# RWKV-7 mixing in chunks of 64 tokens instead of 32, and a reordered VectorE queue in sparse attention

## The chip, the cores and the metric

One core of a Trainium2 chip runs the whole network. The metric is the device time of one execution in microseconds (us), median of the runs. TensorE is called PE in the profile, its weight loads PEld, VectorE is DVE, ScalarE is ACT, GpSimd is POOL and SyncE is SP.

## The reference

A trunk of four layers over 256 tokens of width 1024, float32 in and out. Each layer adds a token mixer's output to the residual stream and then a conv-gated MLP's. The mixers are: layers 0 and 3 sparse attention, layer 1 RWKV-7, layer 2 a state-space layer. Two of them matter here.

Sparse attention: a light indexer (8 heads) scores keys for each query, the best 64 keys are kept, and 16 heads of 64 dimensions attend to those only, causal in blocks of 64. The softmax is over the kept keys.

RWKV-7: for each of 16 heads a 64x64 state goes through the tokens:

```python
sa = einsum('bhij,bhj->bhi', state, -kk_t)
state = state * w_t + sa[..., None] * (kk_t * a_t) + v_t[..., None] * k_t
y = einsum('bhij,bhj->bhi', state, r_t)
```

## The kernel before

Everything is float32 and lies in SBUF with features on the partitions. The dense products split weights and activations into a rounded part and a rest (x_high, x_low) and add three matmuls (`product`, L371 to L373). A weight tile goes through the ring in SBUF; ACT rounds it (`round_weights`, L346), and DVE (half 0) and POOL (half 1) compute the rest (`rest_of_weights`, L354). The five engines' queues are written out by hand, and they meet at semaphores.

Attention (`dsa_pe`, `dsa_act`, `dsa_dve`, `dsa_pool`): the projections k, q, v are four weight tiles each. The attention is cut into 8 units (`UNIT`), each a tile of 128 queries with four heads; a unit has 128 keys (first query tile) or 256. For a unit PE computes `scores` (L863), DVE adds the bias of the chosen keys and takes the row maximum (`mask`, L1131, L1138, L1141), ACT takes exponentials and row sums (`exps`, L1013), DVE inverts the sums (`invert`, L1154), POOL multiplies (`normalise`, L1222), PE transposes (`turn`, L874), ACT copies (`copy_turned`, L1021), and at the end PE multiplies with v (`values`, L894). The scores and turns stand between the projections of q and v. DVE's queue also holds the normalisation of k (`k_norm`, L1095 reciprocal and L1097), the indexer's weighing (L1107) and the top-64 search (`take`, L1116, L1117), and the weight splits `split(s, i)`, each of which makes the rest of the tile two places later, for which PE's projection waits.

RWKV (`rwkv_pe`, `rwkv_act`, `rwkv_dve`): after projections the decays are summed within a chunk of CH = 32 tokens, and scaled factors for every head stand in `big`. The core (PE lines L1381 to L1495) works on four groups G of two head pairs, two groups at a time in turn (`by_groups`: each step for G and then for G+1). In a group there are four blocks w (head pair and half of the tokens), each with four chunks i on strips of 32 partitions, and two heads h. The steps are: `natural` (transpose the factors so that tokens are on partitions), `products` (chunk by chunk inner products, then masked by DVE), `akv`, then the inverse of a triangular 32x32 matrix, doubled in NLEV = 4 levels. A level is `z_product` (L1437), a transposition by matmul with the identity (`turned_t`, L1423), a mask on DVE (L1759), `t_product` (L1448) and an add on DVE (L1769). Then `last_turn`, `solve` (L1464), `outputs` (L1479) and `transitions` (L1495). `chunks` on DVE (L1789, L1792) makes for every chunk a 64x64 transition and an input in `PT_all`. The scan over chunks (L1513 on PE, L1807 on DVE) goes through NCH = 8 chunks, of which 6 steps depend on each other, one DVE instruction for each head and step. At the end the carried state is multiplied in (y, L1526), and the head norm, gate and output projection follow. In this part POOL only splits the weights of "o".

## Time and profile before

| | us |
|---|---|
| median of 3 runs | 1887.64 |
| lowest, highest | 1884.44, 1900.17 |
| the profiled execution, its time | 1886.29 |
| its span in the profile | 1884.6 |
| PE, DVE, ACT, POOL busy in the span | 1578.8, 1061.0, 752.6, 704.0 |

The time of an execution is a little longer than the span in the profile. An engine's busy time is the union of its instructions; a PE record is one matmul instruction, and PEclk is the clock that the chip granted, where 1.00 is 2.4 GHz and 0.50 is 1.2 GHz.

### The profile page before, as it was taken

To read this page: it belongs to the slowest core of one execution; us is meant where nothing else is said; L and a number is where in the kernel's file an instruction comes from. 1 tells how busy PE (TensorE), PEld (TensorE's weight loads), DVE (VectorE), ACT (ScalarE), POOL (GpSimd) and SP (SyncE) were. 2 spreads that over 40 slices of the span, in tenths; PEclk is the share of its full clock that TensorE was granted. 3 is DMA by queue.
4 is the path that set the end of the run, shared out by engine and by line. 5 is a ranking of instruction groups with operands and counts; after the bars stand their busy time and mean duration, and the time that the engine had idled before them with its cause. 6 is when DMAs were issued, how large, how long until landed. Compare 5 with 4: busy or idle time off the path is not lost.

```text
span 1884.6 us, 39207 instructions
## 1 busy us (share of the span) xinstructions
PE 1578.8 (84%) x16992; PEld 1453.9 (77%) x16992; DVE 1061.0 (56%) x1541; ACT 752.6 (40%) x1196; POOL 704.0 (37%) x344
## 2 busy tenths in 40 slices
PE   6888899989974644669998649698999898789999
PEld 5787899977864544569997537498999797689998
DVE  3763477544711216556776895845774358336762
ACT  3454555424110101125553313145654344636653
POOL 5233277620000000035773590033676322426763
PEclk8998899998985655689999869799999998889999
DMA  4442355533420000136555100043555533224553
GB/s 133 135 135 68 119 186 187 177 114 112 134 69 5 4 5 2 45 96 157 186 181 164 46 1 1 0 135 113 181 188 176 160 116 125 96 90 157 182 187 123
DMA packets 213052, 211.58 MB, mean 112 GB/s; under 512 B 12272, under 2 KB 211872, under 8 KB 212896
## 3 DMA queue, kind: packets, MB, share of 16 engines
q1 hardware_dynamic: 210784, 206.65, 34.1%
q0 software_dynamic: 1056, 2.19, 0.7%
q8 instruction: 125, 2.05, 0.5%
q10 hardware_dynamic: 1056, 0.43, 0.1%
q14 instruction: 31, 0.25, 0.0%
HBM read 208.21 MB, written 1.05 MB: 111 GB/s over the span
## 4 chain that ended last, share of the span: by engine, by line
PE 74%; DVE 13%; issue 7%; ACT 4%; ACTq 1%; POOL 1%; DMA 0%; DVEq 0%; POOLq 0%
PE psum L371 14%; PE psum L372 14%; PE psum L373 14%; PE psum L641 6%; PE psum L455 4%; PE psum L643 3%; PE psum L391 2%; DVE work L1807 1%; DVE work L2143 1%; ACT w_high L346 1%; PE psum L2093 1%; DVE work L1095 1%; PE psum L2092 1%; PE psum L1526 1%; DVE work L1107 1%
## 5 line engine op out<-in xcount | busy, mean ns | idle before, releaser
L354 POOL TENSOR_TENSOR w_low<-ring,w_high 128x1024 fp32r<-128x1024 f32 (+1 forms) x184 | 510.6, 2776 | 1090.8 <-ACT w_high L346 1090.7
L371 PE MATMUL psum<-x_high,w_high 128*128 128x256 f32 x2048 | 596.2, 291 | 59.5 <-issue 31.0
L372 PE MATMUL psum<-x_low,w_high 128*128 128x256 f32 x2048 | 590.2, 288 | 0.0
L373 PE MATMUL psum<-x_high,w_low 128*128 128x256 f32 x2048 | 590.0, 288 | 0.0
L346 ACT ACTIVATE w_high<-ring 128x1024 fp32r<-128x1024 f32 (+1 forms) x368 | 361.7, 1034 | 337.9 <-PE psum L373 184.5
L371 PEld LDWEIGHTS psum<-x_high,w_high 128*128 128x128 f32 x2048 | 404.3, 197 | 67.5 <-issue 51.2
L372 PEld LDWEIGHTS psum<-x_low,w_high 128*128 128x128 f32 x2048 | 404.7, 198 | 1.0 <-issue 1.0
L373 PEld LDWEIGHTS psum<-x_high,w_low 128*128 128x128 f32 x2048 | 404.2, 197 | 0.0
L354 DVE TENSOR_TENSOR w_low<-ring,w_high 128x1024 fp32r<-128x1024 f32 (+1 forms) x184 | 228.3, 1242 | 193.1 <-ACT w_high L346 192.9
L726 DVE SCALAR_TENSOR_TENSOR work<-psum,par,work 128x255 f32<-128x255 f32 (+1 forms) x352 | 145.4, 475 | 155.1 <-ACT work L670 155.1
L641 PE MATMUL psum<-inner,w_high 128*128 128x512 f32 x528 | 189.1, 402 | 7.4 <-DVE w_low L354 7.4
L670 ACT ACTIVATE work<-psum,par 128x256 f32<-128x256 f32 x176 | 89.8, 560 | 209.9 <-PE psum L373 209.9
L643 PE MATMUL psum<-inner,w_low 128*128 128x256 f32 x528 | 149.2, 283 | 0.0
L641 PEld LDWEIGHTS psum<-inner,w_high 128*128 128x128 f32 x528 | 100.3, 190 | 32.6 <-DVE w_low L354 7.7
L736 DVE TENSOR_TENSOR work<-work 128x512 f32<-128x512 f32 x44 | 121.9, 2771 | 3.2 <-ACT work L675 3.2
L643 PEld LDWEIGHTS psum<-inner,w_low 128*128 128x128 f32 x528 | 100.8, 191 | 0.0
L455 PE MATMUL psum<-work,ring 128*128 128x256 f32 x384 | 83.2, 379 | 0.0
L455 PEld LDWEIGHTS psum<-work,ring 128*128 128x128 f32 x384 | 73.0, 190 | 10.3 <-issue 0.5
L694 POOL TENSOR_TENSOR inner<-work,inner 128x512 f32 (+1 forms) x44 | 74.9, 1705 | 0.0
L391 PE MATMUL psum<-work,mean_all 128*128 128x256 f32 x128 | 38.9, 470 | 15.1 <-ACT work L383 14.3
L372 PE MATMUL psum<-inner,w_high 128*128 128x256 f32 x176 | 49.8, 283 | 0.0
L371 PE MATMUL psum<-inner,w_high 128*128 128x256 f32 x176 | 49.8, 283 | 0.0
(317 smaller groups left out, 2211.5 us busy)
## 6 DMA issues: line engine op xcount, KB each, us to landing
ring<-in_ffn_w_up_dram SPq DMA_DIRECT2D x88, 1024.0 KB, 5.1
ring<-in_ffn_w_down_dram SPq DMA_DIRECT2D x32, 1024.0 KB, 5.1
ring<-in_dsa_w_in_dram SPq DMA_DIRECT2D x28, 1024.0 KB, 5.2
ring<-in_ffn_w_down_dram SPq DMA_DIRECT2D x16, 768.0 KB, 4.8
ring<-in_rwkv_w_rkv_dram SPq DMA_DIRECT2D x12, 1024.0 KB, 5.1
ring<-in_dsa_w_out_dram SPq DMA_DIRECT2D x8, 1024.0 KB, 5.1
ring<-in_s_w_glu_dram SPq DMA_DIRECT2D x8, 1024.0 KB, 5.5
ring<-in_rwkv_w_out_dram SPq DMA_DIRECT2D x4, 1024.0 KB, 5.2
```

What stands on the lines that cost most here:

```text
L346: act.activation(high, raw, ACT.Copy).then_inc(sem("w_rounded", b), 1)
L354: eng.tensor_tensor(low, raw, high.bitcast(F32), ALU.subtract).then_inc(sem("w_split", b), 1)
L371: pe.matmul(out_, lhs[0], rhs[0], start=start, stop=False, skip_group_check=True)
L372: pe.matmul(out_, lhs[0], rhs[1], start=False, stop=False, skip_group_check=True)
L373: return pe.matmul(out_, lhs[1], rhs[0], start=False, stop=stop, skip_group_check=True)
L391: mm = pe.matmul(banks[7][:, 0:T], mean_all[:, :], sq[n % 2][:, c, :], start=c == 0, stop=c == DC - 1)
L455: mm = pe.matmul(out_, parts[b][:, k, b * P:(b + 1) * P], x[:, k, :], start=start, stop=stop, skip_group_check=True)
L641: pe.matmul(banks[bank][:, :], high[:, k, :], inner[:, :, c, :], start=first, stop=False, skip_group_check=True)
L643: mm = pe.matmul(banks[bank][:, 0:T], low[:, k, :], inner_high[:, c, :], start=False, stop=last, skip_group_check=True)
L670: act.activation(conv[:, j % 3, h, b, :], bank_of(key)[:, b * T:(b + 1) * T], ACT.Identity, bias=col("ffn_conv_b", c + L * 2 * FC, r), sca ...
L726: dve.scalar_tensor_tensor(out=row, in0=bank[:, b * T:(b + 1) * T - lag], scalar=col("ffn_conv_w", c + (L * 3 + tap) * 2 * FC, r), in1=row ...
L736: dve.tensor_tensor(gated[:, j % 3], conv[:, j % 3, 0], conv[:, j % 3, 1], ALU.mult).then_inc(sem("gated_done"), 1)
```

## The change

In RWKV the chunk is 64 tokens. A group now has two strips i of 64 partitions, so a 64x64 block per head and chunk, and every matmul of the core uses tiles of 64x64 in place of 32x32 or 32x64; the doubling has five levels. `turned_t` uses real 128x128 transpositions, four for a group, each of two head pairs' blocks together, and ACT copies the result at each level (before, DVE's mask instruction took it along). `outputs` and `transitions` become one step, `results`. The chunk decay is no longer multiplied in by DVE after the transitions and in the scan: POOL multiplies it into copies of two factors (`b_tail`, `k_tail`) and into the identity (`decay_eye`) before the core, and natural waits for the first two. The scan has two dependent steps, with one DVE instruction for four head pairs. Masks are laid out anew (`blocks` holds 8, `level_masks` is gone), and some ACT and DVE evictions are split or joined accordingly.

In attention `mask` is four `tensor_tensor_reduce` per unit (bias and row maximum in one) in place of two adds and one reduction; `normalise` is on DVE behind the reciprocal, and POOL only splits weights; `k_norm` and the masks take other places in DVE's queue, `rs_k` has four buffers, `scores` and `turn` stand elsewhere between the projections, and `values(g)` starts as soon as its own units and quarter of v are there, the first two between projections. ACT's `exps`, `copy_turned` and `evict_v` are reordered to match.

Of the diff, its core (indentation reduced by eight; in the new functions of the RWKV part only added and kept lines stand, since the old ones are printed above; masks, copies and constants are left out):

```diff
-CH = 32
+CH = 64
 NCH = T // CH
+NLEV = 5
...
-        pe.wait_ge(sem("pt_copied"), before(NU) + since("pt_copied", L))
-        if g == 0:
-            pe.wait_ge(sem("v_ready"), 4 + since("v_ready", L))
-        bank = banks[2 + g]
+        last = max(u for u in range(NU) if unit(u)[1] == g)
+        pe.wait_ge(sem("pt_copied"), before(last + 1) + since("pt_copied", L))
+        pe.wait_ge(sem("v_ready"), g + 1 + since("v_ready", L))
+        if g == 1:
...
     scores(2)
     project_tokens(pe, (L, "v", 0), x_parts, lambda: (q_sum(3), turn(0), scores(3)))
     turn(1)
-    project_tokens(pe, (L, "v", 1), x_parts, lambda: (turn(2), scores(4)))
+    scores(4)
+    project_tokens(pe, (L, "v", 1), x_parts, lambda: (turn(2), scores(5)))
     turn(3)
-    scores(5)
-    project_tokens(pe, (L, "v", 2), x_parts, lambda: scores(6))
-    turn(4)
-    project_tokens(pe, (L, "v", 3), x_parts, lambda: (scores(7), turn(5)))
-    turn(6)
+    scores(6)
+    project_tokens(pe, (L, "v", 2), x_parts, lambda: (turn(4), scores(7)))
+    turn(5)
+    values(0)
+    project_tokens(pe, (L, "v", 3), x_parts, lambda: (turn(6), values(1)))
     turn(7)
-    for g in range(GROUPS):
...
-        w = 2 * nk * P
-        for b in range(2):
-            dve.tensor_tensor(
-                att[:, u % 2, b * w:(b + 1) * w].rearrange("p (h k) -> p h k", h=2),
-                banks[2 + b][:, 0:w].rearrange("p (h k) -> p h k", h=2),
-                bias[qt].unsqueeze(1).to_broadcast([P, 2, nk * P]),
-                ALU.add).then_inc(sem("att_masked"), 1)
-        dve.wait_ge(sem("att_masked"), 2 * (u + 1) + since("att_masked", L))
+        w = nk * P
         r = unit_cols4(u)
-        then(dve.tensor_reduce(row_max[:, r], att[:, u % 2, 0:512 * nk].rearrange("p (h k) -> p h k", h=HG),
-                               AX_X, ALU.max))
+        for i in range(HG):
+            dve.tensor_tensor_reduce(
+                out=att[:, u % 2, i * w:(i + 1) * w], in0=banks[2 + i // 2][:, i % 2 * w:(i % 2 + 1) * w],
+                in1=bias[qt], scale=1.0, scalar=TAKEN, op0=ALU.add, op1=ALU.max,
+                accum_out=row_max[:, u * HG + i:u * HG + i + 1]).then_inc(sem("att_masked"), 1)
+        dve.wait_ge(sem("att_masked"), HG * (u + 1) + since("att_masked", L))
         dve.wait_ge(sem("q_scale"), g // 2 + 1 + since("q_scale", L))
         dve.scalar_tensor_tensor(out=neg_max[:, r], in0=row_max[:, r], scalar=-1.0, in1=q_scale[:, q_cols(u)],
...
-    def invert(u):
+    def normalise(u):
         dve.wait_ge(sem("exp_done"), HG * (u + 1) + since("exp_done", L))
         r = unit_cols4(u)
-        dve.reciprocal(recip[:, r], row_sum[:, r]).then_inc(sem("sums_ready"), 1)
+        then(dve.reciprocal(recip[:, r], row_sum[:, r]))
+        p = prob[:, u % 2, 0:512 * unit(u)[2]].rearrange("p (h k) -> p h k", h=HG)
+        dve.tensor_tensor(p, p, recip[:, r].unsqueeze(2).to_broadcast([P, HG, unit(u)[2] * P]),
+                          ALU.mult).then_inc(sem("prob_normed"), 1)
...
     split("k", 0)
-    k_norm(0)
     weigh(0)
     split("k", 1)
+    k_norm(0)
     take(0, 4)
-    k_norm(1)
     split("k", 2)
     take(0, 4)
     chosen(0)
     weigh(1)
-    k_norm(2)
     split("k", 3)
     take(1, 4)
-    k_norm(3)
     split("q", 0)
+    k_norm(1)
+    split("q", 1)
     take(1, 4)
     chosen(1)
-    split("q", 1)
     scale_q(0)
+    mask(0)
     split("q", 2)
-    mask(0)
     mask(1)
+    k_norm(2)
     split("q", 3)
-    invert(0)
+    normalise(0)
     mask(2)
-    invert(1)
+    normalise(1)
+    k_norm(3)
+    scale_q(1)
     mask(3)
-    invert(2)
+    normalise(2)
     split("v", 0)
-    scale_q(1)
     mask(4)
-    invert(3)
+    normalise(3)
+    mask(5)
+    normalise(4)
     split("v", 1)
-    mask(5)
-    invert(4)
     mask(6)
-    invert(5)
+    normalise(5)
+    mask(7)
+    normalise(6)
     split("v", 2)
-    mask(7)
-    invert(6)
+    normalise(7)
     split("v", 3)
-    invert(7)
...
     def natural(G):
+        if G < 2:
+            pe.wait_ge(sem("bonus_done"), 4)
+            pe.wait_ge(sem("tails_done"), 2)
+        else:
+            pe.wait_ge(sem("p_done"), 2 * (G - 1))
+            pe.wait_ge(sem("q_done"), 2 * (G - 1))
         for s in range(3):
             for w in range(4):
+                hp, t = 2 * G + w // 2, w % 2
+                x = (b_tail[:, hp, 2 * t:2 * t + 2, :], k_tail[:, hp, 2 * t:2 * t + 2, :],
+                     big[:, hp, 3, t * P:(t + 1) * P])[s]
+                pe.transpose(bank4(G)[s][:, w * P:(w + 1) * P], x, ident[:, :])
+        for t in range(TT):
+            for i in range(2):
+                at = (2 * t + i) * P
+                for x in range(2):
+                    mm = pe.matmul(bank4(G)[3][strip(x), at:at + P], big[:, 2 * G + x, 0, tokens(t, i)], ident[:, :],
+                                   start=True, stop=True)
+        mm.then_inc(sem("nat_full"), 1)
+    def products(s):
+        def run(G):
+            if s == 1:
+                pe.wait_ge(sem("nat_done"), 4 * (G + 1))
             for w in range(4):
+                for i in range(2):
+                    hp, c = 2 * G + w // 2, tokens(w, i)
+                    a_at, r_at = hp * 4 * T + c.start, 4 * 2048 + hp * T + c.start
+                    for h in range(2):
+                        r = half_rows(h)
+                        both = flat[r, a_at:a_at + 2 * (r_at - a_at)].rearrange("p (x c) -> p x c", x=2)[:, :, 0:CH]
+                        mm = pe.matmul(bank4(G)[2 * h + s - 1][strip(i), w * P:(w + 1) * P], big[r, hp, s, c], both,
+                                       start=True, stop=True)
+            mm.then_inc(sem("products_full"), 1)
+        return run
+    def first_t(G):
+        pe.wait_ge(sem("products_masked"), masked(0, G))
+        for w in range(4):
+            for i in range(2):
+                hp, c = 2 * G + w // 2, tokens(w, i)
                 for h in range(2):
                     r = half_rows(h)
+                    mm = pe.matmul(bank4(G)[2 * h][strip(i), w * CH:(w + 1) * CH], big[r, hp, 0, c], big[r, hp, 1, c],
+                                   start=True, stop=True)
         mm.then_inc(sem("products_full"), 1)
...
     def turned_t(G):
         p = G % 2
+        for t in range(TT):
+            for h in range(2):
+                at = (2 * t + h) * P
+                mm = pe.transpose(bank4(G)[2][:, at:at + P], Tm[p][:, t, h].rearrange("p x n -> p (x n)"), ident[:, :])
+        mm.then_inc(sem("turned_full"), 1)
     def z_product(l):
         def run(G):
             p = G % 2
             if l == 0:
                 pe.wait_ge(sem("base_done"), G + 1)
+                pe.wait_ge(sem("akv_done"), 2 * (G + 1))
             else:
                 pe.wait_ge(sem("t_added"), level(l - 1, G))
+            turned_t(G)
+            for t, h, x, i in every():
+                w = 2 * x + t
+                mm = pe.matmul(bank4(G)[i][strip(x), (2 * t + h) * CH:(2 * t + h + 1) * CH],
+                               MM[p][strip(i), w, h, AT, :], Tm[p][strip(i), t, h, x, :], start=True, stop=True)
+            mm.then_inc(sem("z_full"), 1)
         return run
     def t_product(l):
         def run(G):
             p = G % 2
+            pe.wait_ge(sem("z_done"), level(l, G))
+            pe.wait_ge(sem("turned_done"), turns(l, G))
+            for t, h, x, i in every():
+                mm = pe.matmul(bank4(G)[x][strip(i), (2 * t + h) * CH:(2 * t + h + 1) * CH],
+                               TmT[p][strip(x), t, h, i, :], Zm[p][strip(x), i, t, h, :], start=True, stop=True)
             mm.then_inc(sem("t_full"), 1)
         return run
     def last_turn(G):
         pe.wait_ge(sem("t_added"), level(NLEV - 1, G))
+        turned_t(G)
     def solve(G):
         p = G % 2
+        pe.wait_ge(sem("turned_done"), turns(NLEV, G))
+        for t, h, x, i in every():
+            mm = pe.matmul(bank4(G)[x][strip(i), (2 * t + h) * P:(2 * t + h + 1) * P], TmT[p][strip(x), t, h, i, :],
+                           XA[p][strip(x), t, i, h].rearrange("p s d -> p (s d)"), start=True, stop=True)
         mm.then_inc(sem("m_full"), 1)
+    def results(G):
         p = G % 2
         pe.wait_ge(sem("m_done"), G + 1)
         for w in range(4):
+            for h in range(2):
+                for i in range(2):
+                    mm = pe.matmul(bank4(G)[i][half_rows(h), w * P:(w + 1) * P], M12[p][strip(i), w, h, 0, :],
+                                   MM[p][strip(i), w, h, BR:BN + 1, :], start=True, stop=True)
+        mm.then_inc(sem("rp_full"), 1)
+        m2 = [M12[p][:, w, :, 1] for w in range(4)]
+        k, v = (KV[p][:, s] for s in range(2))
+        for w in range(4):
+            for at, lhs, rhs, start in ((0, m2[w], MM[p][:, w, :, BR], True), (0, v[:, w], MM[p][:, w, :, KR], False),
+                                        (HALF, MM[p][:, w, :, BN], m2[w], True), (HALF, k[:, w], v[:, w], False)):
                 for h in range(2):
+                    for i in range(2):
+                        mm = pe.matmul(bank4(G)[2 + i][half_rows(h), w * P + at:w * P + at + HALF],
+                                       lhs[strip(i), h, :], rhs[strip(i), h, :], start=start, stop=not start)
+        mm.then_inc(sem("yq_full"), 1)
     levels = [f(l) for l in range(NLEV) for f in (z_product, t_product)]
+    by_groups([natural, products(1), products(2), first_t, akv, *levels, last_turn, solve, results])
+    pe.wait_ge(sem("p_done"), DC)
     pe.wait_ge(sem("q_done"), DC)
...
-                pe.wait_ge(sem("state_done"), 8 * (2 * (c - 2) + q + 1))
+                pe.wait_ge(sem("state_done"), 2 * (2 * (c - 2) + q + 1))
...
 def rwkv_pool(pool, L):
+    pool.wait_ge(sem("factors_done"), 3)
+    pool.wait_ge(sem("decay_ready"), 1)
+    decay = chunk_decay[:, :, :].unsqueeze(3).to_broadcast([P, DC, NCH, HALF])
+    for dst, s in ((b_tail, 1), (k_tail, 2)):
+        pool.tensor_tensor(dst, big[:, :, s, :].rearrange("p h (c s) -> p h c s", c=NCH), decay,
+                           ALU.mult).then_inc(sem("tails_done"), 1)
+    pool.wait_ge(sem("factors_done"), 4)
+    pool.tensor_tensor(decay_eye, head_eye[:, :].unsqueeze(1).unsqueeze(1).to_broadcast([P, DC, NCH, HALF]), decay,
+                       ALU.mult).then_inc(sem("eyes_done"), 1)
+    pool.wait_ge(sem("p_done"), DC)
     for i in range(NSPLIT):
...
+    def z_mask(l):
+        def run(G):
+            p = G % 2
+            dve.wait_ge(sem("z_full"), level(l, G))
+            dve.tensor_tensor(Zm[p].rearrange("p i t h n -> p i (t h) n"),
+                              group_banks(G)[:, 0:2, 0:T].rearrange("p i (u n) -> p i u n", u=4),
+                              blocks[:, 3 + l, :].unsqueeze(1).unsqueeze(1).to_broadcast([P, 2, 4, CH]),
+                              ALU.mult).then_inc(sem("z_done"), 1)
         return run
     def t_add(l):
         def run(G):
             p = G % 2
             dve.wait_ge(sem("t_full"), level(l, G))
+            x = Tm[p].rearrange("p t h x n -> p x (t h) n")
+            dve.tensor_tensor(x, x, group_banks(G)[:, 0:2, 0:T].rearrange("p x (u n) -> p x u n", n=CH), ALU.add).then_inc(sem("t_added"), 1)
         return run
+    def rp(G):
+        dve.wait_ge(sem("rp_full"), G + 1)
+        dve.wait_ge(sem("eyes_done"), 1)
         for x in range(2):
             hp = 2 * G + x
+            each = group_banks(G)[:, 0:2, x * T:(x + 1) * T].rearrange("p i (t s c) -> p t i s c", t=TT, s=2)
+            rr = rT[:, hp, :].rearrange("p (t i c) -> p t i c", t=TT, i=2)
+            dve.tensor_tensor(rr, rr, each[:, :, :, 0, :], ALU.add).then_inc(sem("r1_done"), 1)
+            dve.tensor_tensor(PT_all[:, hp, 0].rearrange("p (t i) j -> p t i j", t=TT), each[:, :, :, 1, :],
+                              decay_eye[:, hp].rearrange("p (t i) j -> p t i j", t=TT),
                               ALU.add).then_inc(sem("p_done"), 1)
+    levels = [f(l) for l in range(NLEV) for f in (z_mask, t_add)]
...
-            for i in range(4):
-                hp = 4 * q + i
-                for h in range(2):
-                    r = half_rows(h)
-                    dve.scalar_tensor_tensor(out=PT_all[r, hp, 1, c, :],
-                                             in0=banks[2 * q + h][r, i * HALF:(i + 1) * HALF],
-                                             scalar=chunk_decay[r, hp, c:c + 1], in1=PT_all[r, hp, 1, c, :],
-                                             op0=ALU.mult, op1=ALU.add).then_inc(sem("state_done"), 1)
+            for h in range(2):
+                r = half_rows(h)
+                state = PT_all[r, 4 * q:4 * q + 4, 1, c, :]
+                dve.tensor_tensor(state, state, banks[2 * q + h][r, 0:T].rearrange("p (i j) -> p i j", i=4),
+                                  ALU.add).then_inc(sem("state_done"), 1)
     yc, root = slot_view(8, DC, T), slot_view(10, DC, T)
     for i in range(NSPLIT):
```

## Rows read from the trace of the kernel before

**Rows 1.** The page's part 4: shares of the chain that ended last, by engine.
```profile
PE 74%; DVE 13%; issue 7%; ACT 4%; ACTq 1%; POOL 1%; DMA 0%; DVEq 0%; POOLq 0%
```
**Rows 2.** Busy time by stage.
```profile
core 0: us, PE busy (x) PEld busy (x) DVE busy (x) ACT busy (x) POOL busy (x), PEclk, DMA share, GB/s
30.00:203.00 173.00, 150.81 (x1188) 141.11 (x1187) 92.89 (x156) 85.94 (x162) 54.83 (x26) 0.92 0.34 109
537.00:726.00 189.00, 101.87 (x6320) 90.43 (x6320) 37.86 (x75) 19.59 (x37) 0.00 (x0) 0.59 0.02 5
604.00:630.00 26.00, 15.97 (x896) 14.07 (x896) 3.99 (x8) 3.75 (x7) 0.00 (x0) 0.50 0.02 4
630.00:634.00 4.00, 3.88 (x47) 3.40 (x51) 2.48 (x4) 0.00 (x0) 0.00 (x0) 0.50 0.02 4
636.00:640.00 4.00, 3.57 (x182) 3.09 (x180) 0.00 (x0) 3.27 (x7) 0.00 (x0) 1.00 0.02 4
...
1505.00:1678.00 173.00, 150.24 (x1175) 140.51 (x1175) 90.83 (x148) 84.92 (x159) 55.29 (x26) 0.91 0.35 109
```
**Rows 3.** PE's costliest group in 537 to 726 us: busy, mean ns, idle before.
```profile
L1423 PE MATMUL psum<-blocks,work 32*32 32x32 f32 x1280 | 20.2, 245 | 20.9 <-issue 20.9
```
**Rows 4.** The chain of waits, 572 to 578 us: start, length, what.
```profile
572.17 2.18 issue
...
576.30 1.78 issue
```
**Rows 5.** DMA queues: packets, MB, share of 16 engines.
```profile
q8 instruction: 125, 2.05, 0.5%
```
**Rows 6.** The chain of waits at the start of the core.
```profile
539.26 1.01 PE psum L1385 x32
540.27 1.46 PE psum L1381 x12
```
**Rows 7.** PE's timeline behind the core: start, length, instructions, idle before.
```profile
727.86 1.97 PE L1513 MATMUL psum<-work 64*64 64x64 f32 x32 [2.58 <-DVE work L1792]
...
759.39 21.30 PE L1526 MATMUL psum<-work 64*64 64x32 f32 x224 [3.92 <-DVE work L1807]
```
**Rows 8.** PE's timeline in the state-space layer.
```profile
1137.01 0.41 PE L2092 MATMUL psum<-work 128*128 128x32 f32 x2
...
1137.68 0.41 PE L2092 MATMUL psum<-work 128*128 128x32 f32 x2
...
1139.20 0.39 PE L2080 MATMUL psum<-work 128*128 128x128 f32 x2
...
1139.53 0.39 PE L2080 MATMUL psum<-work 128*128 128x128 f32 x2
```
**Rows 9.** DVE's timeline in the scan over chunks.
```profile
729.10 30.23 DVE L1807 SCALAR_TENSOR_TENSOR work<-psum,chunk_decay,work 64x64 f32<-64x64 f32 x96 [1.29 <-PE psum L1513]
```
**Rows 10.** DVE's timeline ahead of the core.
```profile
534.09 1.49 DVE L1731 TENSOR_TENSOR work<-psum,work 128x512 f32<-128x512 f32 x2 [18.23 <-PE psum L1364]
```
**Rows 11.** Waits in 52 to 178 us: total, times, longest.
```profile
PE psum L874 <- POOL work L1222: 10.9, 3, 4.8
```
**Rows 12.** PE's timeline in the first attention layer.
```profile
94.21 0.55 PE L371 MATMUL psum<-x_high,w_high 128*128 128x256 f32 x1 [6.64 <-DVE w_low L354]
```
**Rows 13.** Groups of 52 to 205 us, by form: busy, mean ns, idle before.
```profile
L1095 DVE RECIPROCAL work<-work 128x512 f32<-128x512 f32 x4 | 13.4, 3353 | 2.8 <-ACT work L954 2.7
...
L1222 POOL TENSOR_TENSOR work<-work 128x1024 f32<-128x1024 f32 x4 | 8.5, 2116 | 10.3 <-DVE work L1154 10.3
...
L1013 ACT ACTIVATION_READ_ACCUMULATOR work<-work 128x1 f32 x32 | 6.1, 189 | 0.0
...
L1131 DVE TENSOR_TENSOR work<-psum,work 128x512 f32<-128x512 f32 x8 | 5.1, 682 | 4.2 <-PE psum L863 4.2
L1138 DVE TENSOR_REDUCE work<-work 128x4 f32<-128x1024 f32 x4 | 4.9, 1220 | 0.1
...
L1131 DVE TENSOR_TENSOR work<-psum,work 128x256 f32<-128x256 f32 x8 | 3.0, 410 | 5.5 <-PE psum L863 5.5
```

303 lines of the change are left out of this document (106 added, 197 removed).

## The prediction

> **What bounds the kernel now.** I read the page's chain first [rows 1]: TensorE carries 74% of it, so the question in each stage is whether TensorE works or waits. The table by stage [rows 2] separates the two stages that the change touches. In the RWKV core (537 to 726 us) TensorE is busy for only 101.87 of 189 us, at a granted clock of 0.59, and no other engine is near its limit (DVE 37.86, ACT 19.59). In the two attention layers (30 to 203 and 1505 to 1678 us, alike to 0.6 us of busy time) it is busy for 150.8 of 173 us at 0.92.
>
> The groups of the core say what it waits for: the costliest, L1423, idled 20.9 us and all of it is "issue" [rows 3], a wait for nothing that the profile shows. The chain of waits [rows 4] has the pattern: a gap of 2.18 us, a burst, a gap of 1.78 us. From the end of one gap to the end of the next (574.35 to 578.08) is 3.73 us, whatever work lies between. The instruction queue moved 2.05 MB in 125 packets [rows 5], 16.4 KB each; the window holds 6320 matmul records and as many weight loads [rows 2]. 189 us by 6320 is 29.9 ns for a pair, and 3.73 us at that rate is 125 pairs, 250 instructions; 16.4 KB by 250 is 66 bytes each. So each gap is TensorE waiting for its own instructions to arrive, and the core costs about 0.0299 us for each pair, however small the matmul is.
>
> The Trainium skill ("Runtime: NRT & Kernel Launch", Instruction fetch mechanics) says that the sequencer fetches blocks of 256 instructions ahead, and that the crossing is mostly hidden. The trace agrees on the block and not on the hiding; by the page, fewer instructions would save nothing of these gaps, and the sum would lose its largest term.
>
> **The core's instructions.** Each fp32 matmul is two records, a transposition one. Per group of two head pairs the new core has 12 + 16 (natural), 64 (two products), 32 (first_t), 32 (akv), 5 x (4 + 32 + 32) (levels, one more than before), 4 (last turn), 32 (solve), 32 + 128 (results): 692 records, 2768 over four groups. At 0.0299 us that is 83 us of fetch for 189 before.
>
> **The core's passes.** Bigger tiles have to be paid for in the array. A full transposition takes 0.122 us in a run of 12 (1.46 us), and quarter-width passes over the same 128 columns, rotated through four column tiles, 0.032 us (1.01 us for 32) [rows 6]: a pass costs its share of the array when the tiles rotate. The new 64x64 tiles are quarters too, four in rotation: 0.031 us with 128 columns, 0.0155 with 64. Per group: 36 transpositions x 0.122 = 4.4; 16 halves x 0.061 = 1.0; 128 quarter passes with 128 columns x 0.031 = 4.0; 512 with 64 columns x 0.0155 = 7.9. That is 17.3, 69 us for four groups at the 2.4 GHz level and 138 at 1.2. No row shows four 64x64 tiles. The nearest, L1513, alternates two of them at the low level: 32 passes in 1.97 us, 0.062 each [rows 7]; with that price for every pair of passes the 64-column ones cost the double of mine. The other end is L1526, which stays on one tile: 0.095 us with 32 columns [rows 7]. I take the rotation, because L1513 fits it: halved to the high level it is 0.031, twice 0.0155, as two quarters in rotation should give.
>
> **The clock.** The core stood at 0.50 where bursts and gaps alternated, even with TensorE busy for 15.97 of 26 us (604 to 630), and was at 1.00 again by 636, after four dense microseconds (630 to 634) [rows 2]. The new core at the low level would need 138 us for instructions that arrive in 83: it would have no gaps, so the clock would rise. At the high level it needs 69 of 83 us. I expect the high level mostly, with some stretches low: 6 us.
>
> **The chain inside a level.** After z, DVE masks 512 PSUM columns (0.68 us, [rows 13]) while ACT copies the transposed T; then t, then an add of the same size. With two groups interleaved, the other group's 36 or 32 records take about 1 us of fetch and cover 0.68 us and the hop. Not covered: start and end of each of the two group pairs (four ACT copies before the products, masks, M copy, result copies before the next natural), some 5 us each: 10 us. Core: 83 + 10 + 6 = 99, against 190 to the first state matmul at 727.86. Minus 91.
>
> A second rule goes against the change: the Trainium skill ("TensorEngine Tiling (Array Packing)", Key Properties) says that changing the tiling mode drains TensorE. The new levels go from 64x64 tiles to full transpositions and back, some 14 times a group. The trace agrees: L2092 and L2093, which alternate between full and 32-wide tiles, take 0.67 us for four records (1137.01 to 1137.68), L2079 and L2080, all full, 0.33 for three [rows 8]. That is 0.115 us a switch, 6 us for 56 switches, which fits under the fetch; at the low level it would be on top.
>
> **State and y.** The scan over chunks is six steps of 16 VectorE instructions, 96 in 30.23 us [rows 9]. Now it is two steps of four, each over 256 columns, 0.41 us by [rows 13]; with four batches of 16 passes (1.0 us each by [rows 7]) partly beside them: 5.5 us for 31.5. Minus 26. The y matmuls go from 224 to 96 passes with 64 columns for 32, still on one tile at a time: between 0.095 us (columns free) and 0.19 (all of it columns), 9 to 18 us for 21.3 [rows 7]. I take 0.123, twice L1513's 0.062 for one tile in place of two, 12 us: minus 9.
>
> **POOL's part.** The tails are two POOL multiplications of 2048 columns and must land before natural(0). POOL took 2.1 us for 1024 columns [rows 13]: 4.2 to 6 us each, started when the factors are ready, before an idle stretch of 18.23 us on DVE [rows 10], in which TensorE still projects. Hidden; if it were not, natural would wait up to 12 us. The decay_eye product follows and is needed only by the first results. The "o" splits queue behind it, and now wait for p_done; POOL was idle there before [rows 2].
>
> **Attention.** TensorE waited 10.9 us for POOL's normalise in three stalls [rows 11] and 6.64 us for a DVE weight split [rows 12], queued behind k_norm, whose reciprocal alone is 3.35 us [rows 13]. With k_norm(0) after weigh(0) and the others later, that split comes about 7 us earlier, and the first stall goes. Normalise moves to DVE: 4 x 0.41 and 4 x 1.2 us at most, some 7 us more on an engine with 80 us free, while the hop over POOL goes. Values(0) and (1) move between projections, and the tail behind the last projection holds one turn and two values instead of two turns and four. The stretches at 0.92 mean about 28 us at half speed, of which perhaps 5 come back. Sum at most 24 us a layer. What is late next: scores(3) and (4) wait for masks that stand behind k_norm(2) and (3); laid out by hand that gives back about 8. I take 16 a layer, 32 for two, between 0 and 24 each.
>
> The fused mask is worth nothing in this sum. Before: 2 x 0.68 + 1.22 = 2.6 us for a unit with 256 keys [rows 13]; after: 4 x 0.41 = 1.6, plus four reads of the accumulator if each is an instruction, as it is on ACT at 0.19 us [rows 13]: 2.4.
>
> The Trainium skill ("VectorE: DVE Perf Modes", Two Vector instructions with no wait between them) says that an operation which also writes out its accumulator is two instructions. No row of DVE shows it here; by the page the unit is 2.4 us, without it 1.6.
>
> **Sum.** 1886.3 us (span 1884.6 and 1.7 around it) - 91 - 26 - 9 - 32 = 1728; the median of the runs is 1.3 us above the profiled one, so I leave 1728.
>
> **Rivals.**
> A, the forecast: 1728, chance 0.60.
> B, the clock stays at the low level through the core. For it: 604 to 630 was at 0.50 with TensorE 61% busy. Against: no gaps are left there. Core 138 + 10 + 6 = 154: 1783. Chance 0.15.
> C, only two of four 64x64 tiles overlap, L1513's price. Per group 4.4 + 1.0 + 8.0 + 15.9 = 29.3, 117 us at the high level, core 133: 1762; at the low level 234, core 250: 1879, no gain. Chances 0.08 and 0.04.
> D, attention gains nothing because DVE, now with normalise, takes POOL's place as the one waited for: 1760. Chance 0.08.
> E, slower than before: no 64x64 tiles overlap, L1526's price. 0.12 us for 2048 passes with 64 columns and 0.2 for 512 with 128 make 348, with the transpositions over 380 us: core about 390, 2019. It decides from a core of 257 us on, where all the rest is eaten. Against it is L1513. Chance 0.05.
>
> **Numbers.** Range 1690 (fetch alone in the core, 24 us a layer, y at 9) to 1790 (B, D): holds nearly all of A and D, most of B, and C at the high level, about 0.8. A measurement of this kernel tells about 1% from no change. Faster by over 1%: 0.93; within 1%: 0.03 (most of C low); slower: 0.04.
>
> **What would show it.** TensorE's records in the core fall from 6320 to 2768, and it lasts near 100 us. The gaps marked issue are still there, but shorter; if they are gone and the clock is 0.50, it is B. A run of 64-column passes should step at 16 ns (31 low); 31 at the high level is C. DVE's L1807 group shrinks from 96 to 8 instructions. In attention TensorE's waits on POOL disappear, and waits on the DVE mask appear. The prediction is wrong if the core is above 150 us or below 80.

## The result, and the profile after

The kernel after takes 1737.13 us (median of 4, 1735.1 to 1741.02) where the kernel before takes 1886.81 us (median of 4, 1884.44 to 1900.17). The ratio is 0.920, with a 95% interval of 0.915 to 0.925: faster by 8%. The forecast was 1728 us in a range of 1690 to 1790. The profiled execution took 1735.1 us, with a span of 1733.3.

To see where the time went I cut both traces at the end of the same matmuls (line 391, which sum the squares for each normalisation). Each row is the difference of two such ends in one profiled execution, in us; two further kernels, told of below, stand beside them.

| stage | before | after | attention part alone | RWKV part alone |
|---|---|---|---|---|
| attention, first | 184.2 | 166.8 | 166.8 | 184.2 |
| MLP | 199.1 | 199.0 | 198.2 | 199.1 |
| RWKV | 437.1 | 302.6 | 429.5 | 302.9 |
| MLP | 211.8 | 213.9 | 213.4 | 212.2 |
| state space | 238.0 | 254.1 | 240.8 | 242.3 |
| MLP | 201.7 | 204.2 | 202.4 | 201.7 |
| attention, second | 186.7 | 168.0 | 167.1 | 183.4 |

The RWKV layer gave 134.5 us and the attention layers 17.4 and 18.7. Together that is 170.5, but the profiled executions differ by only 151.2 (1886.3 to 1735.1). The rest was given back, 16.1 us of it in the state-space layer, which the change doesn't touch.

**The core.** It now lasts from 523.0 to 617.8 us, 94.8 us to the first state matmul instead of 190. Busy time of TensorE by stretch, the granted clock behind it:

```profile
core 0: us, PE busy (x), PEclk, DMA share, GB/s
523.00:540.00 17.00, 13.82 (x352) 0.93 0.01 3
540.00:560.00 20.00, 18.25 (x653) 0.97 0.02 4
560.00:580.00 20.00, 16.61 (x564) 1.00 0.01 3
580.00:600.00 20.00, 16.61 (x673) 1.00 0.01 4
600.00:617.80 17.80, 13.48 (x556) 1.00 0.01 4
```

In [rows 2] the same work had the clock at 0.50 for long stretches, and TensorE idle for almost half of the time. The chain of waits in one level (from one VectorE mask L1789 to the next) answers to [rows 4]:

```profile
541.34 0.70 DVE work L1789
542.04 0.04 issue
542.09 0.69 PE psum L1463 x32
542.78 0.59 PE psum L1438 x4
543.37 0.62 PE psum L1452 x32
543.99 0.59 PE psum L1438 x4
544.58 0.67 PE psum L1452 x32
545.27 0.70 DVE work L1789
```

The gaps of about 2 us are gone from the levels; what the chain still names issue there is 0.04 us. Over the whole core TensorE waits 4.1 us for issue, where it waited 84.1 us before (the sums over its lines). A level of both groups takes 3.93 us (541.34 to 545.27). It holds 2 x (4 + 32 + 32) = 136 records, so 0.0289 us each: nearly the old price of 0.0299 a pair, though no gap shows. TensorE is busy for 3.58 of the 3.93 us and waits about 0.33 for VectorE's mask. A run of 32 records with 64 columns takes 0.62 to 0.69 us of the chain, 0.019 to 0.022 each with its two ends; inside the run four records start every 0.058 us, 0.0146 each. The instruction queue moved 1.56 MB, where [rows 5] have 2.05:

```profile
q8 instruction: 95, 1.56, 0.4%
```

**State and y.** The timeline behind the core (start, busy time, engine, line, shapes, number of records, idle before), against [rows 7, 9]:

```profile
617.81 1.15 PE L1517 MATMUL psum<-work 64*64 64x64 f32 x32 [1.41 <-ACT work L1638]
618.60 1.77 DVE L1824 TENSOR_TENSOR work<-work,psum 64x256 f32<-64x256 f32 x4 [4.33 <-PE psum L1517]
619.52 2.02 PE L1517 MATMUL psum<-work 64*64 64x64 f32 x32 [0.56 <-DVE work L1824]
620.61 1.85 DVE L1824 TENSOR_TENSOR work<-work,psum 64x256 f32<-64x256 f32 x4 [0.24 <-PE psum L1517]
```

The scan is over in 4.7 us (617.81 to 622.5), with 8 VectorE instructions where there were 96. The 96 records of y take 7.9 us, 0.083 each, at a granted clock of 0.50.

**Attention.** TensorE's waits in the first layer (24 to 191 us: total, times, longest), against [rows 11, 12], and VectorE's groups for the mask, against [rows 13]:

```profile
PE psum L864 <- DVE work L1136: 5.1, 4, 1.9
PE psum L371 <- DVE x_low L410: 3.8, 1, 3.8
PE psum L875 <- DVE work L1157: 0.4, 1, 0.4
```

```profile
L1136 DVE CUSTOM_DVE_ANT_0 work<-psum,work 128x256 f32<-128x256 f32 x16 | 5.8, 415 | 0.2 <-PE psum L864 0.2
L1136 DVE CUSTOM_DVE_ANT_0 work<-psum,work 128x128 f32<-128x128 f32 x16 | 3.6, 280 | 0.0
L1136 DVE DVE_READ_ACCUMULATOR2_ANT work<- 128x1 f32 x32 | 2.6, 82 | 0.0
```

The 10.9 us for GpSimd and the 6.6 for the weight split are gone, and waits for the mask (5.1 us) have appeared.

**The state-space layer.** Its loop over the groups keeps TensorE busy without a break in both kernels. The granted clock is another. Before (ten microseconds a row; the loop begins about 1135):

```profile
1126.80:1136.80 10.00, 7.37 (x31) 0.53 0.00 0
1136.80:1146.80 10.00, 10.00 (x70) 1.00 0.00 0
1146.80:1156.80 10.00, 9.35 (x67) 1.00 0.01 2
```

After, at the same distance from the layer's start:

```profile
976.30:986.30 10.00, 7.30 (x30) 0.50 0.00 0
986.30:996.30 10.00, 10.00 (x41) 0.50 0.01 2
996.30:1006.30 10.00, 10.00 (x42) 0.50 0.00 0
1006.30:1016.30 10.00, 10.00 (x44) 0.54 0.00 0
1016.30:1026.30 10.00, 10.00 (x72) 1.00 0.01 2
```

The engine stays at the 1.2 GHz level for nearly 30 us of unbroken work and gets through 42 records in ten microseconds instead of 70. By these rows that cost some 12 us, most of the 16.

### The profile page after: what moved, and what is told of

It is laid out like the page before. It is cut to its first block, busy times and chain, and to the rows that moved or that the text cites. A ratio compares the mean times of both kernels' runs of the same rounds, so it can differ in the third digit from the quotient of the medians.

```text
span 1733.3 us, 31655 instructions
## 1 busy us (share of the span) xinstructions
PE 1538.7 (89%) x13184; PEld 1411.1 (81%) x13184; DVE 1073.8 (62%) x1557; ACT 767.0 (44%) x1228; POOL 688.9 (40%) x328
## 3 DMA queue, kind: packets, MB, share of 16 engines
q8 instruction: 95, 1.56, 0.4%
## 4 chain that ended last, share of the span: by engine, by line
PE 76%; DVE 14%; issue 4%; ACT 3%; POOL 1%; DMA 1%; ACTq 1%; DVEq 0%; POOLq 0%
PE psum L371 15%; PE psum L373 15%; PE psum L372 15%; PE psum L641 7%; PE psum L455 5%; PE psum L643 3%; DVE w_low L354 2%; PE psum L391 2%; PE psum L2108 2%; DVE work L2158 1%; PE psum L2107 1%; ACT w_high L346 1%; DVE work L406 1%; PE psum L2095 1%; PE psum L1341 1%
## 5 line engine op out<-in xcount | busy, mean ns | idle before, releaser
L354 POOL TENSOR_TENSOR w_low<-ring,w_high 128x1024 fp32r<-128x1024 f32 (+1 forms) x184 | 510.7, 2776 | 883.3 <-ACT w_high L346 883.2
L354 DVE TENSOR_TENSOR w_low<-ring,w_high 128x1024 fp32r<-128x1024 f32 (+1 forms) x184 | 253.0, 1377 | 191.0 <-ACT w_high L346 190.5
L2107 PEld LDWEIGHTS psum<-work 128*128 128x128 f32 x128 | 25.6, 249 | 36.3 <-issue 36.3
L1672 POOL TENSOR_TENSOR work<-work,chunk_decay 128x2048 f32<-128x2048 f32 x2 | 7.5, 3761 | 115.6 <-DVE chunk_decay L1742 115.6
```

The costliest lines, as they stand in the source:

```text
L354: eng.tensor_tensor(low, raw, high.bitcast(F32), ALU.subtract).then_inc(sem("w_split", b), 1)
```

## The experiments

Twelve kernels ran, timed beside the kernel before, whose medians in the three sittings were 1884.78, 1883.75 and 1883.26 us. Since the state-space layer jumps by 16 us from kernel to kernel, I judge an edit first by its own stage in the profiled execution and only then by the median. Stages that nobody had touched tell how far that holds: the old first attention layer took 183.4 to 184.2 us in four kernels, the new one 166.8 to 168.1 in five; the second 183.4 to 186.7 and 167.1 to 168.2.

### The two parts one at a time

Attention part alone (all hunks between the semaphore counts and the end of `dsa_pool`):

> The kernel before with the attention part of the change alone (fused mask, normalisation on VectorE, reordered engines), RWKV in blocks of 32 as before. Theory (the two parts are independent): both attention layers gain what they gained in the kernel after, 17.4 and 18.7 us, so the time is 1887 - 36 = 1851 us, and the RWKV layer stays at 437 us, the state-space layer at 238 us with TensorE's granted clock back at 1.00 some 60 us before its sweeps over the groups end. Rival (the state-space layer's added 16 us come from the attention part, by another phase of the work that follows it): the state-space layer is at 254 us here and the time at 1867 us.

Measured: 1847.53 us (ratio 0.982, interval 0.975 to 0.990), 37 us less. State-space layer 240.8 us.

RWKV part alone (all other hunks). Against the kernel after, the attention's hunks are taken back, and GpSimd's third table is counted with the first two:

```diff
-                dve.wait_ge(sem("eyes_done"), 1)
+                dve.wait_ge(sem("tails_done"), 3)
```

> The kernel before with the RWKV part of the change alone, attention as before (POOL's third table is counted on the semaphore of the first two). Theory: the RWKV layer takes 303 us instead of 437, and nothing else moves: 1887 - 134 = 1753 us, and with the added 16 us of the state-space layer, if these come with the RWKV part, 1769 us. Rival (the 16 us belong to a phase that only both parts together meet): 1753 us, state-space layer at 238 us.

Measured: 1751.64 us (0.928, 0.924 to 0.933), 133 us less. State-space layer 242.3 us.

So each part does in its own layers what it does in the kernel after (table above), and they are independent there. 37.3 and 133.1 sum to 170.4, which would make 1714; together they make 1737. In the profiled executions neither part alone slows the state-space layer by 16 us, so that so far the rival of the second expectation fits (a phase that only both meet). A single profile can't exclude it, though: the attention part's four executions lie between 1841.11 and 1865.33 us.

### Is it the number of instructions?

One edit takes records out of the kernel before without touching its block size; the other puts records into the kernel after without adding a column of work.

In the kernel before (the Z and T copies follow suit):

```diff
-                    for w, i in blocks_of():
-                        mm = pe.matmul(bank4(G)[i][strip(w), (2 + h) * CH:(3 + h) * CH], Tm[p][strip(i), w, h, :],
-                                       blocks[strip(i), 9, :], start=True, stop=True)
+                    mm = pe.transpose(bank4(G)[h][:, 2 * P:3 * P], Tm[p][:, :, h], ident[:, :])
```

> The kernel before, blocks of 32, where the 32 small matmuls that turn T in each level and at its end become 2 full transpositions; VectorE copies the turned blocks with an instruction of its own behind the mask of Z (8 levels of 4 groups hold one such copy more for each of 16 level-groups). 600 matmuls of two records each go. Theory (the fetch of instructions binds the core at 0.0299 us a record): 1200 x 0.0299 = 36 us less, core 190 to 154 us, time about 1851 us, issue still the largest gap. Rival (the chain of PE and VectorE binds, and the small matmuls lie beside it): VectorE's added copies lengthen each chain by 0.4 us, 16 x 0.4 = 6 us more or nothing, 1887 to 1893 us.

In the kernel after, the Z product (the T product likewise):

```diff
-                        mm = pe.matmul(bank4(G)[i][strip(x), (2 * t + h) * CH:(2 * t + h + 1) * CH],
-                                       MM[p][strip(i), w, h, AT, :], Tm[p][strip(i), t, h, x, :], start=True, stop=True)
+                        for n in (0, CH // 2):
+                            at = (2 * t + h) * CH + n
+                            mm = pe.matmul(bank4(G)[i][strip(x), at:at + CH // 2], MM[p][strip(i), w, h, AT, :],
+                                           Tm[p][strip(i), t, h, x, n:n + CH // 2], start=True, stop=True)
```

> The kernel after, where each matmul of the Z and T products (64 columns) is two of 32 columns: the same work in 640 more matmuls, 1280 more records. Theory (fetch costs 0.0299 us a record wherever it is denser than the work): a level of two groups holds 264 records instead of 136 and takes 264 x 0.0299 = 7.9 us instead of 3.93, ten such levels 40 us more, time about 1777 us, and issue gaps come back in the levels. Rival (a level is bound by the chain of products and VectorE's masks, columns count and not instructions): 3.9 us a level as now, time 1737 us to 1745 us. Between: a pass of 32 columns costs what one of 64 does, then 64 more passes a product at some 0.02 us give 2.5 us more a level and group, seen as busy PE and not as issue.

Measured: with full turns 1856.5 us (0.986, 0.980 to 0.992); the RWKV layer went from 437.1 to 400.4 us, 36.7 less. The core alone lost 39.9 us (190.1 to 150.2) for 1240 records fewer (6320 to 5080), 0.032 us a record, while TensorE's busy time in it stayed at 101 us (101.9 and 100.7): all of it came out of the gaps. The theory's size holds (36), and the rival (nothing, or 6 us more) falls.

With halves 1764.24 us (0.934, 0.928 to 0.940); the RWKV layer went from 302.6 to 343.0, 40.4 more for 1280 records more, 0.032 a record. The theory's size holds here too (40), and the rival of no change falls. But this run is the weaker one. Its core is 36.6 us longer (94.8 to 131.4), and 27.5 of these are TensorE's own busy time (78.8 to 106.3), since a record of 32 columns costs about what one of 64 does. That much the case "between" had forecast (2.5 us a level, here 3.58 to 6.02 busy). The rest is what instructions that come late add: the waits for issue in the core rise from 4.1 to 16.6 us. The chain in a level shows the gaps back:

```profile
568.27 1.22 issue
569.49 0.69 PE psum L1467 x28
570.19 0.58 PE psum L1438 x4
570.77 1.12 PE psum L1454 x63
571.90 0.59 PE psum L1438 x4
572.49 0.60 PE psum L1454 x26
573.09 0.14 issue
```

A level takes 7.55 us (562.64 to 570.19, both the first turn of a level) for 264 records, 0.0286 each. Short runs go at 0.018 us a record (63 in 1.12) and then the engine waits. In the kernel after, a level holds nearly as much array work as its fetch needs: transpositions at 0.148 us and records at 0.020 average 0.0275, and the wait for the mask brings that to 0.0289. That is why its gaps have gone while its time per record has not. That the two prices are so near is a coincidence of this kernel.

The traces also hold the packets that bring the instructions. In the core of the kernel before, TensorE has 43 gaps of over 1 us, and every one ends 2.1 to 2.9 us after the start of the latest packet of 16,384 bytes on the instruction queue (q8), of which 49 start in the core, one each 3.8 us. From the end of one gap to the end of the next it starts exactly 128 matmul records in 37 of 42 cases (127 in one, 255 or 256 in the four where a gap is missing). 128 pairs are 256 instructions of 64 bytes, one packet; the prediction's 125 pairs and 66 bytes came from the mean rate. So the gaps are waits for instructions, and not merely as many as the instructions.

The kernel with full turns says what the clock has to do with it. TensorE's busy time in it:

```profile
560.00:580.00 20.00, 13.13 (x743) 0.50 0.02 5
580.00:600.00 20.00, 13.29 (x725) 0.59 0.02 5
```

```profile
578.09 0.69 PE L1422 MATMUL psum<-ident,work 128*128 128x128 f32 x2
578.71 0.39 PE L1435 MATMUL psum<-work 32*32 32x32 f32 x27
580.66 0.65 PE L1435 MATMUL psum<-work 32*32 32x32 f32 x37 [1.56 <-issue]
```

A turn costs 0.31 us there (two in 0.62 us of the chain) and 0.148 in the kernel after, because the clock is at the low level, as in the kernel before. The gain of 37 us came all the same: at 743 records in 20 us the fetch sets the pace at either clock.

### The scan

```diff
-                    for h in range(2):
-                        r = half_rows(h)
-                        state = PT_all[r, 4 * q:4 * q + 4, 1, c, :]
+                    for i in range(4):
+                        for h in range(2):
+                            r = half_rows(h)
+                            state = PT_all[r, 4 * q + i, 1, c, :]
```

> The kernel after, where the scan over the chunks adds the state head by head (8 VectorE instructions of 64x64 a step instead of 2 of 64x256). Theory (VectorE's instructions bind the scan, 96 of them took 31.5 us before, 0.33 us each): the scan's 2 x 2 steps hold 32 of them, 10.5 us instead of 4.7, the RWKV layer 309 us instead of 303, time 1743 us. Rival (the number of steps alone shortened it, six to two): scan stays under 6 us, time 1737 us.

```profile
617.00 6.96 DVE L1825 TENSOR_TENSOR work<-work,psum 64x64 f32<-64x64 f32 x28
618.02 1.12 PE L1517 MATMUL psum<-work 64*64 64x64 f32 x16 [1.67 <-DVE work L1825]
620.02 1.12 PE L1517 MATMUL psum<-work 64*64 64x64 f32 x16 [0.88 <-DVE work L1825]
624.02 4.28 PE L1530 MATMUL psum<-work 64*64 64x64 f32 x51 [2.88 <-DVE work L1825]
```

(The window shown begins and ends inside the first and the last row.) VectorE now works through without a gap, 0.25 us each (28 in 6.96), 32 in 8.0. From the first state matmul (615.21) to the first of y (624.02) the scan takes 8.8 us, against 4.7. So joining the heads is worth 4.1 us of the scan, less than the 5.8 expected, and of the 26.8 us gained the other 22.7 come from two steps in place of six and from the plain addition (0.25 us where the multiplication and addition of [rows 9] took 0.31). The time did not show it: 1728.77 us (0.915, 0.909 to 0.922), with single executions at 1734.99, 1723.89, 1720.6 and 1733.66. The layer as a whole was as long as before the edit (302.8 us), because the projections L1329 and L1341 were 3.3 us quicker, with less of the layer at the low clock (54.6 us for 58.0). The median moved by less than the clock's own steps.

### The attention's parts

Mask and maximum in three instructions a unit instead of four fused ones:

```diff
-                    dve.tensor_tensor_reduce(
+                    dve.tensor_tensor(
...
+                then(dve.tensor_reduce(row_max[:, r], att[:, u % 2, 0:512 * nk].rearrange("p (h k) -> p h k", h=HG),
+                                       AX_X, ALU.max))
```

> The kernel after with the attention mask as before: two adds of two heads each and one reduction for the maximum, in place of four fused instructions a unit. Theory of the prediction (the fused mask is worth nothing): 1737 us, attention layers 167 and 168 us. Rival (by the durations measured after, four fused of 0.415 or 0.280 us with accumulator reads of 0.082 us sum to 12.0 us a layer where adds and reductions took 15.7 us before, and PE now waits for the masks): 3.7 us more a layer, up to 7 us more in all, 1744 us.

Measured: 1722.4 us (0.916, 0.909 to 0.924), but the attention layers took 170.0 and 170.1 us, 3.1 and 2.1 longer. The total is shorter mainly because the state-space layer fell back to 237.7. The fused mask is worth 2 to 3 us a layer: the rival of this run is right for the layers (it had 3.7), though not for the total, and the prediction's "nothing" is wrong.

Normalisation back on GpSimd:

```diff
-                then(dve.reciprocal(recip[:, r], row_sum[:, r]))
+                dve.reciprocal(recip[:, r], row_sum[:, r]).then_inc(sem("sums_ready"), 1)
...
+                pool.tensor_tensor(p, p, recip[:, unit_cols4(u)].unsqueeze(2).to_broadcast([P, HG, nk * P]),
+                                   ALU.mult).then_inc(sem("prob_normed"), 1)
```

> The kernel after with the normalisation of the attention's weights back on GpSimd, between its splits of weights, the reordered sequence of the other engines kept (GpSimd's third RWKV table is counted on the semaphore of the first two). Theory (PE's waits for GpSimd, 10.9 us a layer before, were the largest part of the attention's gain): 8 to 11 us more a layer, attention 177 us, time about 1757 us. Rival (the gain came from the reordering and from the value products drawn into the projections): under 4 us a layer, time under 1745 us.

Measured: 1730.21 us (0.918, 0.912 to 0.923), attention layers 164.7 and 166.4 us: 2.1 and 1.6 shorter, not 8 to 11 longer. Its waits in 90 to 190 us:

```profile
PE psum L864 <- DVE work L1136: 1.4, 1, 1.4
PE psum L875 <- POOL work L1226: 0.8, 1, 0.8
```

GpSimd costs TensorE 0.8 us in the new order where it cost 10.9 in the old one. The move to VectorE is thus a loss, if a small one: without it the mask waits are 1.4 us instead of 5.1. It was the order that took GpSimd's stall away; GpSimd's own queue has another order here too, with the first four normalisations behind its last split for q. The two later kernels with this edit had 166.7 and 165.9 us in the first layer and 166.4 in the second, so the loss is between 1 and 2 us a layer; unchanged first layers differ by 1.3 us between kernels.

Value products behind the last turn again:

```diff
-            values(0)
-            project_tokens(pe, (L, "v", 3), x_parts, lambda: (turn(6), values(1)))
+            project_tokens(pe, (L, "v", 3), x_parts, lambda: turn(6))
             turn(7)
+            values(0)
+            values(1)
```

> The kernel after with all four groups of value products behind the last turn, as before, instead of two of them drawn in beside the last projection. Theory (with 24 passes a group they cover the wait for the last weights' normalisation, some 3 to 5 us a layer): each attention layer 3 to 5 us longer, 171 us; total 1743 to 1747 us where the state-space layer keeps its 254 us. Rival (the last turns wait for nothing by then): under 1 us a layer.

Measured: 1723.99 us (0.914, 0.909 to 0.919; single executions 1711.6 to 1730.97), attention layers 164.4 and 164.6 us, 2.4 and 3.4 shorter. Both theory and rival missed the sign: drawing the value products forward loses a little, by one profiled execution. What is left of the change as the source of the 17 to 19 us a layer is the order of the key normalisations, turns, scores and copies. I didn't take that apart further.

### The state-space layer

The loop issues, for each of four groups of a set, a product on a full tile and one that is 32 columns wide. The edit issues the four of one kind first:

```diff
                 for j in range(4):
                     pe.matmul(banks[4 + i % 2][:, j * S5_N:(j + 1) * S5_N], FT[i % 2][:, c], u, start=True, stop=True)
+                for j in range(4):
                     mm = pe.matmul(banks[6 + i % 2][0:S5_N, c], u, TZ[i % 2][:, c], start=True, stop=True)
```

> The kernel after, where the state-space layer's loop over 16 group sets issues its four state products (full tiles) and then its four output products (32 columns wide) instead of one of each in turn: same instructions, tile shape changed twice a set and not eight times. Theory (the alternation of tile shapes under the half clock keeps TensorE too thin for the clock to rise, and whether it rises at the loop's start hangs on the phase): the granted clock goes to 1.00 within the first 10 us of the loop, the state-space layer takes 238 us or less instead of 254, time 1737 - 16 = 1721 us. Rival (phase alone decides, the order within a set has no part): the clock stays at 0.50 for the loop's first 30 us as in the kernel after, layer 254 us, time 1737 us. Second rival (fewer changes of shape save only their drain): 16 sets x 6 changes at a few tens of ns, under 3 us less.

Measured: 1713.01 us (0.908, 0.903 to 0.914), in four executions from 1711.3 to 1714.24. The layer took 233.8 us instead of 254.1. The same rows as above:

```profile
975.70:985.70 10.00, 7.37 (x39) 0.56 0.00 0
985.70:995.70 10.00, 8.84 (x76) 1.00 0.01 2
995.70:1005.70 10.00, 9.12 (x64) 0.83 0.00 0
1005.70:1015.70 10.00, 10.00 (x86) 1.00 0.01 2
```

The same edit in the kernel before:

> The kernel before with the same grouping of the state-space loop alone. There the granted clock already rose at the loop's start in the profiled execution, layer 238.0 us. Theory (grouping is worth 4 us of drains at the full clock, and 16 us more only where the clock would else stay low): layer 234 us, profiled time about 1881 us, median 1881, and the spread between executions (1880 to 1901 us) shrinks to a few us. Rival (grouping is worth 20 us whatever the clock does): 1865 us.

Measured: 1880.81 us over 10 executions (0.998, 0.995 to 1.000); they lie between 1877.07 and 1884.58, while the 13 of the kernel before in that sitting lie between 1879.9 and 1898.35. The layer took 234.6 us for 238.0, and the spread shrank as the theory had it. So the grouping itself is worth 3.4 us at the full clock, and 20.3 where the clock would have stayed low. The rival (20 us whatever the clock does) falls.

The layer in all fourteen profiled kernels, in us: with the old loop 254.1, 254.1, 254.1, 254.2 and 257.5 (after, scan by head, normalisation on GpSimd, values last, halves), and 237.7, 238.0, 240.8, 242.3 and 242.4 (mask in three, before, attention alone, RWKV alone, full turns); with the grouped loop 233.8, 234.2, 234.6 and 238.8. The old loop has two outcomes, 11.7 us apart at the nearest, with the same code. Only one execution of a kernel is profiled, so what the others did has to be inferred from their times: the kernel with halves took 1777.55 and 1770.46 at a mean clock of 0.920 and 0.924, and 1755.45 and 1758.03 at 0.940 and 0.938, so its executions probably fall on both sides, and the four of the kernel after (1735.1 to 1741.02) probably all on the slow one. None of the four grouped kernels shows the slow outcome, nor do the times of their 22 executions, which lie within 8 us for each kernel. So alternating shapes seem to be needed for it; what picks the outcome is open. I tried no kernel that only shifts the start of the loop.

### A version that beats both

Grouping and the normalisation on GpSimd together:

> The kernel after with two edits that each shortened it alone: the state-space loop's output products grouped behind the state products (24 us less) and the normalisation back on GpSimd (attention layers 2.1 and 1.6 us shorter). Theory (the two touch different layers and add): attention 164.7 and 166.4 us, state-space layer 234 us, time 1713 - 4 = 1709 us. Rival (the phase of the clock in the state-space layer undoes the first once the attention's length moves): state-space layer back at 250 us or more, 1725 us.

And with the two heads of y in turn:

```diff
-                for h in range(2):
-                    for hp in (2 * q, 2 * q + 1):
-                        for c in range(1, NCH):
+                for hp in (2 * q, 2 * q + 1):
+                    for c in range(1, NCH):
+                        for h in range(2):
```

> The same as the run beside it, and the 24 products of each quarter of y alternate between the two heads' tiles instead of finishing one head first. Theory (records of one tile follow at 0.083 us at the half clock because each waits for the last one's columns): in two tiles they take 0.04 to 0.06 us, y's 96 records 4 to 6 us instead of 7.9, time 2 to 4 us less than the run beside it. Rival (y's products are hidden beside VectorE's additions and what follows): same time as the run beside it within 1 us.

Measured: 1707.97 us (0.908, 0.906 to 0.910) and 1709.69 us (0.907, 0.905 to 0.910). The first is 29 us below the kernel after, as its theory says (1709); the two are the fastest kernels here. The value products behind the last turn, which shortened both attention layers, are not in them; the three edits together didn't run. The y products in the two, the first without and the second with the edit:

```profile
618.71 7.29 PE L1542 MATMUL psum<-work 64*64 64x64 f32 x96 [1.31 <-DVE work L1836]
```

```profile
616.27 2.31 PE L1542 MATMUL psum<-work 64*64 64x64 f32 x72 [1.06 <-DVE work L1836]
621.31 1.16 PE L1542 MATMUL psum<-work 64*64 64x64 f32 x24 [2.72 <-DVE work L1848]
```

Two tiles in turn take 0.032 us a record (72 in 2.31) for 0.076 on one; but the granted clock was 0.98 there (616 to 622 us) and 0.61 in the other (618.7 to 626), which alone would make 0.046 of the 0.076 (an estimate; the other run's records that fell at 1.00 started 0.047 apart), so only the step from 0.046 to 0.032 is left to the tiles. Behind them TensorE waits 2.72 us for VectorE's additions (L1848), and the next matmuls start 6.1 us after y's beginning instead of 7.2. The remaining microsecond is not to be seen in the total: rival right, except that the RWKV layer was 4.5 us shorter (296.1 for 300.6) and the two layers behind it, with more time at the low clock, 7.9 longer (MLP 215.5 for 212.2, state space 238.8 for 234.2).

## Why the prediction was right, and where not

- **What bounds the core before: right.** "The core costs about 0.0299 us for each pair": 0.032 a record came out of the core's gaps when records were taken out. The rule of the Trainium skill ("Runtime: NRT & Kernel Launch", Instruction fetch mechanics) that the crossing is mostly hidden does not hold for matmuls this small, as that run and the 43 gaps behind packets of instructions show.
- **Core 99 us: right in size, in part by luck.** It lasted 94.8, with 2768 records as counted. Fetch was set at 83, ends at 10, low clock at 6. Little of the 6 came: the clock was 0.93 up to 540 us and 0.97 to 1.00 behind it. But the 83 isn't what TensorE spent: it was busy for 78.8 us and waited 12 for VectorE and ScalarE and 4.1 for issue. The fetch's sum came near because array work and waits happen to add up to it. Rival B was excluded by the clock.
- **"The gaps marked issue are still there, but shorter": wrong in the levels.** There the chain has 0.04 us of it. The price of a pass was right: 0.0146 us where I had 0.0155, and 0.109 for a transposition in a run where I had 0.122. What I had let vanish under the fetch was the change of tile. Before and behind each turn TensorE loses together about 0.31 us by the records' starts (estimate: 24 turns, 7.4 us; I had 6), so four transpositions take 0.59 us of the chain, 0.148 each. Nor does the other group's work cover the mask wholly: 3.3 us of waits in ten levels. A level's array work and waits thus equal its fetch instead of lying under it. It cost little, since the larger of the two counts.
- **C and E: excluded.** The 64-column pass would have been 0.031 us for C and 0.12 for E.
- **State 5.5 us: right in sum** (4.7), with a price per VectorE instruction of 0.44 us (four in 1.77) and the steps as the main cause.
- **y 12 us: too dear.** 7.9. The 64-column pass on one tile cost 0.083 us at the low clock, less than the 0.095 of a 32-column one before, so my lower bound (9 us) was not one: I had taken a price from a row where the wait was not the columns. In both traces the commonest step from one record to the next on one tile is 0.107 us at the clock of 0.50, with 32 columns as with 64.
- **POOL's part: right.** Its two tails took 3.76 us each, and the first transposition waited for the bonus on VectorE (0.99 us), not for them.
- **Attention 16 us a layer: right** (17.4 and 18.7), **for partly wrong reasons.** The stall for GpSimd did go, the waits for masks came (5.1 us, I had 8 given back), and 5.7 us came from TensorE's shorter busy time in the first layer (157.9 to 152.2), which I had put at 5; the granted clock of the layer rose from 0.91 to 0.97. But "the hop over POOL goes" was no gain: normalising on VectorE loses 1 to 2 us a layer, drawing the values forward another 2 to 3. Which moves of the order made up the rest is not shown.
- **"The fused mask is worth nothing": wrong.** The accumulator's read is an instruction of its own, as the Trainium skill ("VectorE: DVE Perf Modes", Two Vector instructions with no wait between them) has it: the trace has 32 of them beside 32 fused ones. But it takes 0.082 us, and I had priced it by ScalarE's 0.19. A unit of 256 keys is 4 x (0.415 + 0.082) = 2.0 us instead of the 2.4 I had, against 2.6 before, and a layer has 12.0 us of mask work (5.8 + 3.6 + 2.6) where it had 15.7. Taking it back cost 3.1 and 2.1 us.
- **What the sum lacked.** 91 + 26 + 9 + 32 = 158 forecast, 170.5 found in the layers that were changed (95.3 + 26.8 + 13.4 less 1.0 elsewhere in RWKV, and 36.1), 151.2 found in the whole. The forecast is 7 us below the profiled execution and 9 below the median because two errors met, which is luck: I had left 12 us of gain out, and had no term for a layer whose code stays the same. The state-space layer took 16.1 back, the MLPs 3.5. With the loop grouped the time is 1713.

## What to carry to other kernels

Count TensorE's instructions before its columns where tiles are small: in the core before, each record of a small tile cost 0.03 us, whichever clock was granted, because its instructions came no faster. An absence of gaps did not mean that this floor was far: array work and waits had grown up to it. When work ahead of an unchanged stage is shortened, read that stage's granted clock again; a loop that changes tile shape at each matmul can stay at the low level for tens of microseconds, and with like shapes issued together none of four kernels here met that. Judge small edits by their own stage in the trace, since the total moved by up to 20 us for reasons of clock.
